# Four of 22 pairs of upward FFN tiles computed with seven half-size products

## The reference, cut to what matters

```python
def conv_ffn(h, w_up, conv_w, w_down):
    gu = causal_dwconv(h @ w_up, conv_w)
    g, u = jnp.split(gu, 2, axis=-1)
    return (jax.nn.silu(g) * u) @ w_down
```

## Time and profile before

| what | us |
|---|---|
| median of three runs | 1222.25 |
| the profiled execution | 1223.61 |
| its span, first to last instruction | 1221.5 |
| TensorE (PE) busy | 1207.6 (99%) |
| weight loads (PEld) busy | 990.1 (81%) |
| DVE, ACT, POOL busy | 698.6, 612.0, 700.3 |
| granted TensorE clock, mean | 0.999 of full |

### The profile page before, as it was taken

How to read it: one execution, slowest core, us unless ns; L and a number is a source line. 1 busy time by engine, 2 the same in 40 slices (tenths; PEclk the granted TensorE clock), 3 DMA queues, 4 the chain that set the end, 5 groups by cost and what they waited for, 6 DMA issues and landing times.

```text
span 1221.5 us, 18340 instructions
## 1 busy us (share of the span) xinstructions
PE 1207.6 (99%) x6667; PEld 990.1 (81%) x6667; DVE 698.6 (57%) x1239; ACT 612.0 (50%) x1184; POOL 700.3 (57%) x538
## 2 busy tenths in 40 slices
PE   9999999999999999999999999999999999999997
PEld 7977777777888899987887777878888888889886
DVE  5545426757646777745697555445454545966224
ACT  6355535676644344445634656544444444333544
POOL 8673232353269776855484566545655565886842
PEclk9999999999999999999999999999999999999999
DMA  7432222122223333354142223333333333333332
GB/s 236 107 95 73 70 61 61 52 63 77 70 62 103 95 98 94 107 179 116 52 119 58 58 62 96 96 85 104 87 88 102 103 88 80 101 96 117 108 87 69
DMA packets 62432, 112.22 MB, mean 92 GB/s; under 512 B 6856, under 2 KB 11464, under 8 KB 62344
## 3 DMA queue, kind: packets, MB, share of 16 engines
q1 hardware_dynamic: 62200, 111.06, 32.5%
q10 hardware_dynamic: 144, 0.00, 0.0%
HBM read 108.87 MB, written 2.16 MB: 91 GB/s over the span
## 4 chain that ended last, share of the span: by engine, by line
PE 95%; DVE 3%; ACT 1%; issue 1%; POOL 1%; DMA 0%; SPq 0%; DVEq 0%; POOLq 0%; ACTq 0%
PE pb L1101 23%; PE pb L1102 23%; PE pb L1104 23%; PE pb L1154 3%; PE pb L1156 3%; PE pb L1155 3%; PE pb L1310 2%; PE pb L1286 2%; PE pb L1163 2%; PE pb L1253 1%; PE pb L1224 1%; PE pb L1226 1%; PE pb L1225 1%; PE pb L1207 1%; PE pb L1205 1%; PE pb L1275 1%
## 5 line engine op out<-in xcount | busy, mean ns | idle before, releaser
L2684 POOL TENSOR_TENSOR wlo<-raw,whi 128x512 fp32r<-128x512 f32 (+2 forms) x384 | 518.7, 1369 | 333.2 <-ACT whi L1503 332.2
L1101 PE MATMUL pb<-HH,whi 128*128 128x512 f32 x856 | 345.4, 404 | 0.0
L1102 PE MATMUL pb<-HL,whi 128*128 128x512 f32 x856 | 338.5, 395 | 0.0
L1104 PE MATMUL pb<-HH,wlo 128*128 128x512 f32 x856 | 337.5, 394 | 0.0
L1503 ACT ACTIVATE whi<-raw 128x512 fp32r<-128x512 f32 (+2 forms) x384 | 226.1, 613 | 106.9 <-PE pb L1104 55.7
L1101 PEld LDWEIGHTS pb<-HH,whi 128*128 128x128 f32 x856 | 161.3, 188 | 42.2 <-issue 4.6
L1102 PEld LDWEIGHTS pb<-HL,whi 128*128 128x128 f32 x856 | 161.0, 188 | 38.1 <-issue 2.9
L1104 PEld LDWEIGHTS pb<-HH,wlo 128*128 128x128 f32 x856 | 160.9, 188 | 37.4
L1976 DVE TENSOR_TENSOR pb<-pb,rff 128x512 f32<-128x512 f32 x44 | 30.8, 700 | 124.0 <-PE pb L1104 117.6
L1621 ACT ACTIVATE P<-P,stat 128x256 f32<-128x256 f32 (+3 forms) x96 | 50.5, 527 | 78.7 <-DVE stat L2246 57.1
L2684 POOL TENSOR_TENSOR fl<-cv,fh 128x512 fp32r<-128x512 f32 x22 | 28.9, 1314 | 86.4 <-ACT fh L1897 86.4
(11 more groups left out here) (461 smaller groups left out, 2512.2 us busy)
## 6 DMA issues: line engine op xcount, KB each, us to landing
raw<-in_wall SPq DMA_DIRECT2D x368, 256.0 KB, 2.8
raw<-in_wall SPq DMA_DIRECT2D x8, 260.0 KB, 3.2
X<-in_xT SPq DMA_DIRECT2D x8, 256.0 KB, 5.4
X<-in_xT SPq DMA_DIRECT2D x2, 1024.0 KB, 7.6
outT<-PP SPq DMA_DIRECT2D x8, 256.0 KB, 2.5
raw<-in_wall SPq DMA_DIRECT2D x10, 192.0 KB, 2.4
raw<-in_wall SPq DMA_DIRECT2D x9, 128.0 KB, 2.4
cst<-in_cst SPq DMA_DIRECT2D x1, 832.0 KB, 7.6
```

What stands on the lines that cost most here:

```text
L1101: pe.do.matmul(b, hi, xh[k], start=start, stop=False, skip_group_check=tile[0] == "down")
L1102: pe.do.matmul(b, hi, xl[k], start=False, stop=False, skip_group_check=tile[0] == "down")
L1104: m = pe.do.matmul(b, lo, xh[k], start=False, stop=stop, skip_group_check=tile[0] == "down")
L2684: g.do.tensor_tensor(lo, x, hi.bitcast(F32), ALU.subtract).then_inc(*up(name, point))
```

## The change

Pairs j = 6, 9, 12 and 15 of the upward FFN (`UPS`) are computed by seven products. Their weights come as four quarters, and their four weight sums are made by DVE. The token sums and their parts are made once, in four portions, behind pairs j = 1 to 4, in PSUM banks and in buffers that later belong to the pairs 16, 18, 20 and to work space; `product` of the pairs above 15 waits for the last use of those. The order around such a pair is new: all splits up to the last factor S4 stand ahead of the convolution steps of the plain pair in front (j-1). These steps, scaled(1, j-1), taps(0, j-1), swish(j-1) and product(j-2), follow behind the third product, S2, and behind them the split of the first plain unit after the pair. The steps taps(1, j-1) and product(j-1) follow behind the product S3. The low part of S3's factor is made by POOL for these pairs, not by DVE. A tile `cd` takes a third bank. For the products, ACT copies a half bank once per pair and DVE does six additions of 128 x 256.

```diff
+UPS = (6, 9, 12, 15)
+NUP = NGATE + len(UPS)
...
     for j in range(NPAIR):
-        fm("ffn_up", P * j)
-        fm("ffn_up", 2816 + P * j)
+        if j in UPS:
+            fm4(NGATE + UPS.index(j))
+        else:
+            fm("ffn_up", P * j)
+            fm("ffn_up", 2816 + P * j)
...
         for x in FACTORS:
-            self.split_to(self.unit_of[p, x] + LOOK)
+            if not (NGATE <= p < NUP and x == "S2"):
+                self.split_to(self.unit_of[p, x] + LOOK)
             self.add("product7", p, x)
+            if NGATE <= p < NUP and x == "S2":
+                j = UPS[p - NGATE] - 1
+                self.add("scaled", 1, j)
+                self.add("taps", 0, j)
+                self.add("swish", j)
+                self.add("product", j - 1)
+                self.split_to(self.unit_of[p, x] + LOOK)
+            if x == "S3" and NGATE <= p < NUP:
+                self.add("taps", 1, UPS[p - NGATE] - 1)
+                self.add("product", UPS[p - NGATE] - 1)
...
+        sums_of = {j + 1: j for j in range(4)}
         for j in range(NPAIR):
+            if j in UPS:
+                for t in (("ffn", 0, j), ("cd", j), ("ffn", 1, j)):
+                    take(t)
+                self.pair(NGATE + UPS.index(j))
             for half in range(2):
-                take(("ffn", half, j))
-                self.proj(("ffn", half, j), "ffn_up", 2816 * half + P * j)
+                if j not in UPS:
+                    take(("ffn", half, j))
+                    self.proj(("ffn", half, j), "ffn_up", 2816 * half + P * j)
...
+                if half and j + 1 in UPS:
+                    self.split_to(self.unit_of[NGATE + UPS.index(j + 1), "S4"])
+                    continue
                 add("scaled", half, j)
-                if (half, j) != (0, 0):
-                    add("taps", 1 - half, j - 1 + half)
                 if half:
+                    add("taps", 0, j)
                     add("swish", j)
-                elif j:
-                    add("product", j - 1)
+                elif j and j not in UPS:
+                    add("taps", 1, j - 1)
+                    if j + 1 not in UPS:
+                        add("product", j - 1)
+                if j in sums_of and half == 0:
+                    for i in range(2):
+                        take(("ts", sums_of[j], i))
+                    add("t_sums", 3, sums_of[j])
+                elif j in sums_of:
+                    add("t_parts", 3, sums_of[j])
...
+                    a.do.activation(TSU[kp][:, 0:T], xk[kp], ACT.Copy, scale=gain).then_inc(*up("a_t7"))
+                    a.do.activation(ps("ts", kp, 0)[:, H:T], xk[kp][:, H:T], ACT.Copy, scale=gain).then_inc(*up("a_t7"))
+                    a.do.activation(ps("ts", kp, 1), xk[kp + 4], ACT.Copy, scale=vecs("ffn_norm", kp + 4)).then_inc(
+                        *up("a_t7", ("t_scaled", kp)))
...
             def product7(p, x):
-                if p >= NGATE:
+                if kind(p) == "up" and x == "S2":
+                    a.wait_ge(*at("product7", p, x))
+                    a.wait_ge(*at("u3", p - 1))
+                    a.do.activation(U7, ps("ffn", 0, UPS[p - NGATE])[:, 0:H], ACT.Copy).then_inc(*up("a_c7", ("v0", p)))
+                if kind(p) != "gate":
                     return
...
             def product(j):
                 a.wait_ge(*at("product", j))
+                if j > 15:
+                    a.wait_ge(*at("product7", NUP - 1, "S3"))
...
+                if x == "S2":
+                    v.wait_ge(*at("v0", p))
+                    v.wait_ge(*at("product7", p, "S2"))
+                    plus(U7, ab[:, right], U7, ("u2", p))
+                elif x == "S3":
+                    v.wait_ge(*at("product7", p, "S3"))
+                    v.wait_ge(*last("v_c7"))
+                    plus(W8, cd[:, left], U7)
+                    plus(ZU, cd[:, right], U7, ("u3", p))
+                    v.wait_ge(*last("v_c7"))
+                    plus(e[:, right], cd[:, right], W8, ("empty", ("cd", j)))
+                    plus(e[:, left], e[:, left], ZU)
+                elif x == "S4":
+                    v.wait_ge(*at("product7", p, "S4"))
+                    plus(ab[:, right], ab[:, right], W8)
...
-                elif factor[1] == "S3":
+                elif factor[1] == "S3" and kind(factor[0]) != "up":
                     return
...
```

More of the change, by code:

```diff
@@ L72, in quarters @@
         mat, (one, two) = "win", (gm_col(*x) for x in PAIRS[p])
+    elif p < NUP:
+        mat, one, two = "ffn_up", P * UPS[p - NGATE], 2816 + P * UPS[p - NGATE]
     else:
-        mat, one, two = "ffn_dn", 2 * P * (p - NGATE), 2 * P * (p - NGATE) + P
+        mat, one, two = "ffn_dn", 2 * P * (p - NUP), 2 * P * (p - NUP) + P
     return {"A11": (mat, one, 0), "A22": (mat, two, 4), "A21": (mat, two, 0), "A12": (mat, one, 4)}
@@ L139, in plan_units @@
     for j in range(NPAIR):
-        fm("ffn_up", P * j)
-        fm("ffn_up", 2816 + P * j)
+        if j in UPS:
[3 more added lines that the diff above has]
+            fm("ffn_up", 2816 + P * j)
     for x, n in DOWN:
         if x == "pair":
-            fm4(NGATE + n)
+            fm4(NUP + n)
         else:
@@ L171, in __init__ @@
         self.where, self.units, self.unit_of, self.load_of, self.last_load = {}, [], {}, {}, []
-        quarter_of = {(mat, k0, col): (p, x) for p in range(NGATE + 4) for x, (mat, col, k0) in quarters(p).items()}
+        quarter_of = {(mat, k0, col): (p, x) for p in range(NUP + 4) for x, (mat, col, k0) in quarters(p).items()}
         for n, blocks in enumerate(self.loads):
@@ L664, in second @@
                 self.hold(DOWN_BANK["tile"][7], ("down", 7))
-            self.pair(NGATE + n)
+            self.pair(NUP + n)
             add("down_out", 2 * n)
@@ L948, in sums_at, with kind @@
             return S7 if p < NGATE else S8
+        def kind(p):
+            return "gate" if p < NGATE else "up" if p < NUP else "down"
         T_AT = {"S1": 0, "S3": 1, "A22": 2, "S2": 3}
@@ L1004, in build @@
         ffn_work = a3.p
+        sums_places = [(ffn_work, ffn_work + 8 * T)] + [(place[f"fh{j}"], place[f"fl{j}"]) for j in (16, 18, 20)]
+        THU, TLU = ([tensor_at(f"tu{n}{kp}", [P, 2 * T], F32R, sums_places[kp][x]) [:, :] for kp in range(4)]
+                    for x, n in enumerate("hl"))
+        TSU = [tensor_at(f"tus{kp}", [P, 2 * T], F32, sums_places[kp][1])[:, :] for kp in range(4)]
+        ZU = tensor_at("zu", [P, H], F32, 226176)[:, :]
         a3.p += 4 * (4 * T + 64)
@@ L1117, in product7 @@
                 later = []
-                if p < NGATE:
+                if kind(p) == "up":
+                    g, (xhs, xls), (ths, tls), j = 3, (hh, hl), (THU, TLU), UPS[p - NGATE]
+                    tile, half = {"A11": (("ffn", 0, j), 0), "S2": (("ffn", 0, j), 1), "S1": (("cd", j), 0), "S3": (("cd", j), 1),
+                                  "A12": (("ffn", 0, j), 0), "S4": (("ffn", 0, j), 1), "A22": (("ffn", 1, j), 0)}[x]
+                    b, starts = ps(*tile)[:, H * half:H * half + H], x in ("A11", "S1", "A22", "S4")
+                    if x == "A12":
+                        pe.wait_ge(*at("u2", p))
+                    elif x in ("A11", "S1", "A22"):
+                        free(tile)
+                elif p < NGATE:
                     g, (xhs, xls), (ths, tls) = 0, (hh, hl), (TH7, TL7)
@@ L1128, in product7 @@
                 else:
-                    g, (xhs, xls), (ths, tls), q = 1, (FH, FL), (TH8, TL8), p - NGATE
+                    g, (xhs, xls), (ths, tls), q = 1, (FH, FL), (TH8, TL8), p - NUP
                     tile, half = {"A11": (("dn", q, "ab"), 0), "S2": (("dn", q, "ab"), 1), "S1": (("dn", q, "cd"), 0),
@@ L1149, in product7 @@
                         if g:
-                            pe.wait_ge(*at("f_hi", n))
-                            pe.wait_ge(*at("f_lo", n))
+                            pe.wait_ge(*at({1: "f_hi", 3: "h3_hi"}[g], n))
+                            pe.wait_ge(*at({1: "f_lo", 3: "h3_lo"}[g], n))
                     w = slice(P * k, P * k + P)
@@ L1512, in t_sums @@
                             *up("a_t7", ("t_copied", kp, i)))
+                if g == 3:
+                    gain = vecs("ffn_norm", kp)
+                    for i, d in enumerate((kp, kp + 4)):
+                        a.wait_ge(*at("x_ffn", d))
+                        if before["ts", kp, i] is not None:
+                            a.wait_ge(*at("empty", before["ts", kp, i]))
+                    a.wait_ge(*at("full", ("wout", 7)))
+                    a.wait_ge(*at("x_ffn", 7))
+                    a.wait_ge(*at("mix_lo", 7))
+                    a.do.activation(TSU[kp][:, 0:T], xk[kp], ACT.Copy, scale=gain).then_inc(*up("a_t7"))
+                    a.do.activation(ps("ts", kp, 0)[:, H:T], xk[kp][:, H:T], ACT.Copy, scale=gain).then_inc(*up("a_t7"))
+                    a.do.activation(ps("ts", kp, 1), xk[kp + 4], ACT.Copy, scale=vecs("ffn_norm", kp + 4)).then_inc(
```

(48 more changed lines are left out.)

## The result

The changed kernel takes 1227.43 us (median of six runs, 1225.61 to 1229.09) against 1222.26 for the kernel before in the same session. The ratio is 1.0038, with a 95% interval of 1.0025 to 1.0051: slower by 5.2 us, where 3.1 had been forecast. The profiled execution is the shortest of the six, 1225.61 us.

A forecast was written before the change was run, and what follows sets the result against it. TensorE, busy 1207.6 of 1221.5 us, was taken to bound the kernel. Saving -5.0, stalls after pairs +7.6 and token sums +0.5 gave +3.1 on 1222.25: 1225.3 us, range 1217.2 to 1229.5.

The forecast's parts named there:

- What PE saves: Upward FFN pairs: seven products take 9.90 us against 11.16 plain, saving 1.26 us a pair, 5.0 for four.
- Waits inside the pair: Within a seven-product pair: TensorE waits for no factor, cost nothing; bounds 0 and 0.3 us a pair.
- The bound of 0.3 a pair: Upper bound for TensorE's waits inside a pair, as long as the longer single wait on POOL in a streaming stage.
- The wait after the pair: First plain unit behind a pair: low part ready 8.01 us after S2, wanted at 6.12; stall 1.9 us, 7.6 for four.
- the same chain: After S2: ACT's copy, DVE's convolution steps, `fh`, next split, `fl`, POOL's low part; 8.01 us in all.
- The token sums: Behind pairs 1 to 4: added ACT, DVE and POOL work may delay the first seven-product pair; 0.5 us, bounds 0 and 2.
- The sum: Whole kernel: -5.0 + 7.6 + 0.5 = +3.1 us, so 1225.3 us; terms' bounds give 1223.6 to 1229.3.
- unit 7 is not late: Rival: first plain unit after a pair is in time, the saving stays, 1217.2 us; chance 0.25 for gain over 0.2%.
- The stall eats the saving and no more: Rival: behind each pair, stall of 1.2 to 1.7 us, no token-sum lateness, 1222.0 to 1224.0 us; chance 0.25.
- DVE and POOL do slow one another: Rival: in the chain after S2, fused products meet POOL instructions; four pairs grow by 9, 1234 us; chance 0.07.

The follow-up runs named there:

- The version with no wait left: Changed kernel with the split of unit 7 ahead of S2's product and the convolution steps, and pairs 7, 10, 13, 16: 1217.37 us, ratio 0.9956.
- the version with the split first: Changed kernel with only the split of the first plain unit after a pair moved ahead of S2's product and the convolution steps: 1217.7 us, ratio 0.9960.
- the eleven runs of that version: Changed kernel with seven-product pairs 7, 10, 13, 16 in place of 6, 9, 12, 15, order around a pair untouched: 1224.89 us, ratio 1.0019.
- a stand of 5.7 us: Changed kernel with the split of unit 7 still later at pair 6 alone, behind product S3 and product(j-1): 1232.86 us, ratio 1.0082.

## Why the prediction was right

- *What PE saves* (5.0 us): right, a little low. Pair 9 took 900.70 - 890.95 = 9.75 us against 9.90 of the gate pair, so 11.16 - 9.75 = 1.41 a pair, 5.6 in all. The version with no wait left gained 5.3. The Trainium skill's rule of a fixed cost per matmul (TensorE: Matmul & The Clock Gate, section "Wait — 56ns, not 53.3ns?") gave an estimate of 4.7; the measurement lies above both sums.
- *Waits inside the pair* (none): right; the first wait of each pair in the changed kernel comes at the plain unit behind it. The bound of 0.3 a pair came from a row that was misread: `rgl` in the earlier trace rows is the low part of a stream and not of a weight. Nothing else hangs on it.
- *The wait after the pair* (1.9 us each): right to 0.1 at pairs 9, 12 and 15, by the same chain on the same engines, and shown to be the cause: with one split moved, all but 0.7 us of the waits and 9.7 us of time go. About 0.3 of each 1.9 lies already ahead of the unit's first matmul (900.58 to 900.95): ACT's split of it starts only at 900.19, so the high part was late as well, which the layout didn't have.
- *The token sums* (0.5 us): undersized, 1.0. Their loop ran late, but not by more with each pair: against the kernel before, scaled(1, j) on DVE started 2.0, 3.3, 3.4 and 3.5 us later at pairs 1 to 4, and scaled(0, j) in time until pair 5, where it was 1.4 late. The two fused products, 1.42 us in the earlier trace rows, took 2.79 to 2.93 beside POOL's conversions:

```profile
819.31 2.79 DVE L2059 SCALAR_TENSOR_TENSOR cv<-cv,cv 128x512 f32<-128x512 f32 x2
841.64 2.93 DVE L2059 SCALAR_TENSOR_TENSOR cv<-cv,cv 128x512 f32<-128x512 f32 x2
```

The lateness reached PE by a way that I hadn't named. At pair 6 DVE's sum S4 waits for POOL's low part of S1, ACT's split of S4 waits for that sum, and ACT's copy of the half bank, with which the chain starts, stands behind that split (DVE's, then ACT's timeline):

```profile
859.12 1.71 DVE L2090 TENSOR_TENSOR s7a<-raw,s7b 128x512 f32<-128x512 f32 x1 [3.75 <-POOL wlo L2793]
...
860.87 0.63 ACT L1554 ACTIVATE whi<-s7a 128x512 fp32r<-128x512 f32 x1 [4.03 <-DVE s7a L2090]
861.40 0.36 ACT L1587 ACTIVATE u<-pb 128x256 f32<-128x256 f32 x1
```

With S2 over at about 860.2 the copy would have started at 860.4: 1.0 us late, and the wait is 2.9 in place of 1.9. That it comes from the token sums just ahead is shown by the run with one plain pair more, in which the first pair loses 1.9 like the others; which of their steps made POOL late, DVE's slow products or POOL's own low parts of the last portion (2.55 us from 852.27), no run separates.
- *The sum*: the waits are 8.6 us, less 5.6 saved: +3.0 by its terms. That this meets the forecast so closely is luck in part: the saving was 0.6 too low and the token sums 0.5 too low, and the two cancel. The stage itself, from the matmul that ends the norm's sums (794.96 us before, 793.69 after) to the first `fh` matmul (1035.67 and 1037.48), is 3.1 us longer in the profiled execution; its start 1.3 us earlier comes from two shorter waits in the first block, which the change doesn't touch: TensorE gets 0.35 ahead at one for a low weight part and 0.85 at one for a DMA (`PE pb <- DMA decay_qB`, 1.1 us before and 0.2 after). So the forecast of +3.1 is the time of the shortest runs, 1225.6. The median is 1.8 above that. That is the term that was missing: the granted clock, which I took to stay at 1.00 as in the earlier trace rows. It falls behind pair 6's wait in some executions. One profile shows that at 1227.36, with 1.55 us lost; the profile at 1225.61 has a clock of 1.00 there. All eleven runs of the changed kernel lie on three levels, 1225.6 to 1225.9, 1227.4 to 1227.6 and 1229.1, some 1.7 us apart, so most executions seem to hold one such stretch. That the two of 1229.09 hold two of them, or a longer one, was not seen. Two slips in the prediction's numbers don't move the forecast: its bounds end at 1229.3 and its range at 1229.5, and the part of the bounds above 2.4 us is four fifths, (7.0 - 2.4) / 5.6, not two thirds.
- *The rivals*: "unit 7 is not late" describes the version with the split first, not this one. "The stall eats the saving and no more" failed by the waits. DVE and POOL do slow one another, but in the token sums, not in the chain, where POOL was idle as laid out: the fused products took their 1.42 us there.

## What to carry to other kernels

Look-ahead counted in units is worth less time where the units get shorter: five units of 2.79 us cover the convolution, five of 1.41 don't. When work is moved behind a stage's last product, list for each engine what then stands behind it, and put the conversion that TensorE wants next ahead of everything that only has to be done sometime. A wait of TensorE can cost more than itself: where the granted clock fell behind one, 1.3 and 1.55 us came on top.

## What the runs showed of the hardware that was not expected

The clock: behind a stand of 2.9 us, with two matmuls in it, the granted clock fell for 3.4 us in one profiled execution and not in another of the same kernel; behind waits of 1.9 us, four to an execution, the eleven runs of that version stayed within 0.8 us at a mean clock of 0.998; in a stand of 5.7 us it fell before TensorE resumed, and all four runs have a mean clock of 0.994 to 0.996. And DVE's two fused products, each of two SBUF operands, took 1.42 us together alone and 2.6 to 2.9 beside POOL, while its work from PSUM kept its 0.70 and 1.52 there.
